# More buffers for the scores of a retrieval layer, its gate loads in thirds, and a softmax exponential one column later

## The reference, cut to what matters

```python
q = (xb @ peer_wq).reshape(PEER_BLOCK, PEER_HEADS, 2, PEER_HALF)
s = jnp.einsum('thpd,pkd->thpk', q, peer_subkeys).astype(jnp.float32)
sv, si = lax.top_k(s, PEER_TOPK)
cand = sv[:, :, 0, :, None] + sv[:, :, 1, None, :]    # 16 x 16 per head
fv, fi = lax.top_k(cand, PEER_TOPK)
eidx = jnp.take_along_axis(cidx, fi, axis=-1)
gate = jax.nn.softmax(fv, axis=-1).astype(xb.dtype)
act = jax.nn.gelu(jnp.einsum('thkd,td->thk', peer_u[eidx], xb))
return jnp.einsum('thk,thkd->td', gate * act, peer_v[eidx])
```

## Time and profile before

| | us |
|---|---|
| median of 3 runs | 4133.24 (4130.62 to 4139.96) |
| the profiled execution | 4130.32 |
| its span, first to last instruction | 4128.6 |
| TensorE busy in it | 3873.2 |
| columns, first to last matmul | 1758.0 to 3008.0 |
| values, first to last matmul | 3008.0 to 4088.0 |

### The profile page before, as it was taken

The page is one execution under the profiler, slowest core; times in us unless marked ns, Lnnn a source line. Parts: engine busy times, 40 slices in busy tenths (PEclk is TensorE's granted clock), DMA queues, the critical chain, the costliest instruction groups (busy, mean ns, idle before and its releaser), DMA issues.

```text
span 4128.6 us, 62540 instructions
## 1 busy us (share of the span) xinstructions
PE 3873.2 (94%) x24143; PEld 3747.4 (91%) x24143; DVE 2592.3 (63%) x3356; ACT 1327.0 (32%) x1620; POOL 806.3 (20%) x514
## 2 busy tenths in 40 slices
PE   8988988979989979999899998999999999999996
PEld 6788978979967979999899998999999999999996
DVE  3423323351363356678888565666898898989896
ACT  3333211132252123232355322222233333333333
POOL 0000010020000020037300021221433233444430
PEclk9989989989999999999999999999999999999998
DMA  6532322223452222234355798999999999999993
GB/s 225 207 115 57 85 60 72 72 60 81 165 222 72 71 62 72 82 127 146 117 194 210 287 348 321 358 343 370 414 406 405 397 393 407 390 402 396 400 377 134
DMA packets 418864, 941.40 MB, mean 228 GB/s; under 512 B 26404, under 2 KB 299488, under 8 KB 366616
## 3 DMA queue, kind: packets, MB, share of 16 engines
q1 hardware_dynamic: 367136, 565.78, 40.4%
q0 software_dynamic: 51616, 374.19, 22.3%
HBM read 865.84 MB, written 72.77 MB: 227 GB/s over the span
## 4 chain that ended last, share of the span: by engine, by line
PE 65%; DMA 16%; DVE 12%; ACT 3%; issue 2%; SPq 2%; DVEq 1%; POOL 0%; ACTq 0%
PE pp L197 25%; PE pp L1134 15%; DMA p_scr<-sa 9%; PE pp L1184 6%; DMA p_f<-p_scr 5%; PE pt L1184 3%; PE pl L1184 3%; DVE gbuf L1926 3%; PE pt L1108 2%; PE pp L809 2%; DVE v_lo L1949 2%; DVE xs_r L1930 1%; PE pt L809 1%; DVE p_lo L1953 1%; PE pl L809 1%
## 5 line engine op out<-in xcount | busy, mean ns | idle before, releaser
L1134 PE MATMUL pp<-h_hi,ut_hi 128*128 128x384 f32 x2048 | 713.1, 348 | 51.8 <-DVE ut_lo L1832 51.2
L1134 PE MATMUL pp<-h_lo,ut_hi 128*128 128x384 f32 x2048 | 698.1, 341 | 0.0
L1134 PE MATMUL pp<-h_hi,ut_lo 128*128 128x384 f32 x2048 | 696.1, 340 | 0.0
L212 DVE TENSOR_TENSOR w_lo<-raw,w_hi 128x2048 fp32r<-128x2048 f32 x120 | 274.7, 2290 | 424.9 <-ACT w_hi L207 424.9
L1832 DVE TENSOR_TENSOR ut_lo<-u_raw,ut_hi 128x1024 fp32r<-128x1024 f32 x256 | 333.0, 1304 | 285.5 <-ACT ut_hi L1415 283.7
L1490 ACT ACTIVATE v_hi<-v_raw 128x1024 fp32r<-128x1024 f32 x256 | 271.9, 1062 | 690.0 <-PE pp L1184 361.0
L1134 PEld LDWEIGHTS pp<-h_hi,ut_hi 128*128 128x128 f32 x2048 | 392.0, 191 | 56.2 <-DVE ut_lo L1832 55.0
L1949 DVE TENSOR_TENSOR v_lo<-v_raw,v_hi 128x1024 fp32r<-128x1024 f32 x256 | 313.0, 1223 | 130.1 <-ACT v_hi L1490 130.0
L1134 PEld LDWEIGHTS pp<-h_lo,ut_hi 128*128 128x128 f32 x2048 | 391.8, 191 | 0.0
L1134 PEld LDWEIGHTS pp<-h_hi,ut_lo 128*128 128x128 f32 x2048 | 390.9, 191 | 0.0
L207 ACT ACTIVATE w_hi<-raw 128x2048 fp32r<-128x2048 f32 x120 | 229.3, 1911 | 419.7 <-PE pp L197 298.2
(11 more groups left out here) (382 smaller groups left out, 7854.1 us busy)
## 6 DMA issues: line engine op xcount, KB each, us to landing
u_raw<-in_peer_ut SPq DMA_DIRECT2D x256, 512.0 KB, 5.6
v_raw<-in_peer_v SPq DMA_DIRECT2D x256, 512.0 KB, 7.9
p_f<-p_scr SPq DMA_DIRECT2D x256, 192.0 KB, 10.7
raw<-in_w_in SPq DMA_DIRECT2D x24, 1024.0 KB, 5.6
g_scr<-gs POOLq DMA_DIRECT2D x6, 4096.0 KB, 13.3
raw<-in_w_mk SPq DMA_DIRECT2D x16, 1024.0 KB, 4.8
raw<-in_w_mv SPq DMA_DIRECT2D x16, 1024.0 KB, 4.8
raw<-in_w_out SPq DMA_DIRECT2D x16, 1024.0 KB, 6.0
```

The source lines that it names most:

```text
L212: nc.vector.tensor_tensor(w_lo[:, s], raw[:, s], w_hi[:, s].bitcast(F32), ALU.subtract).then_inc(lo_ready, 1)
L1134: last = mm(pp[0][:, d, 0:N], w[:, d, k, :], x[:, k, S:S + N], start=(k == 0 and w is ut_hi and x is h_hi), stop=(k == KC - 1 and w is ut_lo))
```

## The change

- fg becomes fs, four buffers in the place of the seventh gather buffer, from column 56 on (columns 0 to 55 keep fg); sa gets four buffers; f_stored and s_in count per buffer. NG_BUF is 6.
- ScalarE has a loop of its own for the gated columns, and waits for the stores of g_scr ahead of it, since fs lies where the last gate tiles were.
- SP's order in a gated column is now: store of sa, first half of u_raw, store of fs, second half of u_raw, load of sa, one stored column further ahead than before (into the buffer whose store was issued a column ago), a third of the gate loads in three columns of four.
- The exponential stands between columns 26 and 27, and VectorE makes the low parts of column 27 ahead of the subtraction, and those of column 28 alone between normalising and the copies.
- The three lists are turned into three banks, with no wait between them.
- Semaphores of GpSimd's memsets are merged into pool_made and const_ready.

```diff
-NG_BUF = 7
+NG_BUF = 6
+        ijt_bank = [pt[0], pt[1], pp[1][:, 0]]
-        sa = at("sa", TMP + 9728, [P, 2, N])
+        fs = at("fs", Y_HI + 49152, [P, 4, N])
+        sa = at("sa", TMP + 6400, [P, 4, N])
...
+            def fours_part(x, q, k, n):
+                for dst, i in ((g4, q),) + (((a4, k),) if k is not None else ()):
+                    sp.dma_start(dst[x][:, 2 * n:2 * n + 2, :, :], gv[i][:, 2 * n:2 * n + 2]).then_inc(g4_in[x], 16)
...
+            def steady(j, d):
+                b = j * 8 + d if isinstance(j, int) else None
+                s, mid = d % 2, b is None
+                if mid or AHEAD + 2 <= b < 2 * AHEAD + 2:
+                    sp.wait_ge(gm_done, j * 16 + (2 * (d - AHEAD) - 2))
+                    sp.dma_start(p_scr[j * 8 + (d - AHEAD - 2)], sa[:, (d - 2) % 4, :]).then_inc(pa_stored[s], 16)
+                if mid or b + 2 < NK:
+                    sp.wait_ge(t_lo, j * 16 + (2 * d + 1))
+                    sp.dma_start(u_raw[:, s, 0:HD], uv[j * 8 + (d + 2)][:, 0:HD]).then_inc(u_in[s][0], 16)
...
+                if mid or AHEAD + 2 <= b < 2 * AHEAD + 2:
+                    sp.wait_ge(gm_done, j * 16 + (2 * (d - AHEAD) - 3))
+                    sp.dma_start(p_scr[j * 8 + (d - 2)], fs[:, (d - 2) % 4, :]).then_inc(f_stored[(d - 2) % 4], 16)
+                elif b >= AHEAD + 2:
+                    p_store(b - 2)
+                if mid or b + 2 < NK:
+                    sp.wait_ge(t_lo, j * 16 + (2 * d + 2))
+                    sp.dma_start(u_raw[:, s, HD:D], uv[j * 8 + (d + 2)][:, HD:D]).then_inc(u_in[s][1], 16)
+                if mid or AHEAD < b < 2 * AHEAD - 1:
+                    if mid or b >= AHEAD + 3:
+                        sp.wait_ge(pa_stored[1 - s], j * 64 + 16 * ((d - 3) // 2 + 1 - AHEAD // 2))
+                    sp.dma_start(sa[:, (d + 1) % 4, :], s_scr[j * 8 + (d - AHEAD + 1)]).then_inc(s_in[(d + 1) % 4], 16)
+                if d % 4 and (mid or b + 4 < NK):
+                    both = mid or b < 2 * AHEAD - 4
+                    fours_part((d // 4 + 1) % 2, j * 2 + (d // 4 + 1),
+                               j * 2 + (d // 4 + 1 - AHEAD // 4) if both else None, d % 4 - 1)
...
             for x in range(3):
                 src = gw if x == 2 else ij[:, x]
-                if x >= 1:
-                    pe.wait_ge(ijt_out, x)
                 for t in range(ND):
-                    last = turn(pt[0][:, t * P:(t + 1) * P], src[:, t + 1, :], ident[:, :])
+                    last = turn(ijt_bank[x][:, t * P:(t + 1) * P], src[:, t + 1, :], ident[:, :])
                 last.then_inc(ijt_done, 1)
-            pe.wait_ge(ijt_out, 3)
...
+            column(PICK // 2 - 1, 0)
             act.wait_ge(g_sub, 1)
             f(gw[:, :, :], gw[:, :, :], ACT.Exp).then_inc(g_exp, 1)
-            for d in range(2):
-                column(PICK // 2 - 1, d)
+            column(PICK // 2 - 1, 1)
...
+            def gated_gelu(q, d):
+                act.wait_ge(u_done, q * 4 + (d + 1))
+                if not isinstance(q, int) or q > AHEAD // 4:
+                    act.wait_ge(f_stored[d], q * 16 + stored(d, -(AHEAD // 4)))
+                f(fs[:, d, :], pp[0][:, d % 2, 0:N], ACT.Gelu_apprx_tanh).then_inc(ge_done, 1)
...
+            for s in range(2):
+                act.wait_ge(g_stored[s], 16 * ND)
+            for d in range(4):
+                gated_column(AHEAD // 4, d)
...
-            def next_rows(count=1, upto=2 * (PICK - 1)):
+            def next_rows(count=1, upto=2 * PICK):
...
-            while turned[0] < 2 * (PICK - 1):
+            while turned[0] < 2 * PICK:
```

More of the change, by code:

```diff
@@ L487, in program, with stored @@
         u_done, ge_done, gm_done = sem("u_done"), sem("ge_done"), sem("gm_done")
-        f_stored = [sem("f_stored0"), sem("f_stored1")]
-        g4_in, s_in, pa_stored = [[sem(f"{w}{s}") for s in range(2)] for w in ("g4_in", "s_in", "pa_stored")]
+        f_stored = [sem(f"f_stored{s}") for s in range(4)]
+        g4_in, pa_stored = [[sem(f"{w}{s}") for s in range(2)] for w in ("g4_in", "pa_stored")]
+        s_in = [sem(f"s_in{s}") for s in range(4)]
+        def stored(s, n):
+            return 16 * n + (8 * AHEAD if s < 2 else 0)
         def gated_count(b):
@@ L708, in ahead_steady @@
[L708 to L736, removed]
+                    for n in range(3):
+                        fours_part(0, AHEAD // 4, 0, n)
@@ L737, in _ @@
+                    for x in range(2):
+                        sp.wait_ge(f_stored[x], 16 * AHEAD // 2)
+                    for q in range(2):
+                        sp.dma_start(sa[:, q, :], s_scr[q]).then_inc(s_in[q], 16)
                 if b == NK - 2:
@@ L739, in _ @@
                         sp.wait_ge(pa_stored[x], 16 * AHEAD // 2)
-                    for d in range(4):
-                        p_load(0, d)
+                    for n in range(4):
+                        p_load(0, n)
                     sp.wait_ge(t_lo, 2 * (NK - 1))
-                    for d in range(2):
[L744 to L749, removed]
+                    for n in range(2):
+                        v_load(0, 0, n)
+                if mid or AHEAD + 2 <= b < 2 * AHEAD + 2:
[14 more added lines that the diff above has]
+                               j * 2 + (d // 4 + 1 - AHEAD // 4) if both else None, d % 4 - 1)
+            for d in range(8):
+                steady(AHEAD // 8, d)
+            with sp.Fori(AHEAD // 8 + 1, AHEAD // 4 - 1) as j:
+                for d in range(8):
+                    steady(j, d)
+            for b in range(2 * AHEAD - 8, NK):
+                steady(b // 8, b % 8)
             sp.wait_ge(t_lo, 2 * NK)
@@ L761, in _ @@
                     value_loads(0, i, d)
-            for s in range(2):
-                sp.wait_ge(f_stored[s], 16 * NK // 2)
+            for s in range(4):
+                sp.wait_ge(f_stored[s], stored(s, (NK - AHEAD) // 4))
             with sp.Fori(AHEAD // 4, NK // 4) as i:
@@ L1458, in _, with gated_column @@
                     column(i, d)
+            column(PICK // 2 - 1, 0)
             act.wait_ge(g_sub, 1)
             f(gw[:, :, :], gw[:, :, :], ACT.Exp).then_inc(g_exp, 1)
-            for d in range(2):
-                column(PICK // 2 - 1, d)
+            column(PICK // 2 - 1, 1)
             for x in range(3):
                 act.wait_ge(ijt_done, x + 1)
-                f(ijt[:, x, :], pt[0][:, 0:N], ACT.Copy).then_inc(ijt_out, 1)
+                f(ijt[:, x, :], ijt_bank[x][:, 0:N], ACT.Copy).then_inc(ijt_out, 1)
             gate_columns(act, column)
-            with act.Fori(PICK // 2 + 4 * ND, GELU_S) as i:
+            with act.Fori(PICK // 2 + 4 * ND, AHEAD // 2) as i:
                 for d in range(2):
                     column(i, d)
+            def gated_gelu(q, d):
[3 more added lines that the diff above has]
+                f(fs[:, d, :], pp[0][:, d % 2, 0:N], ACT.Gelu_apprx_tanh).then_inc(ge_done, 1)
+            def gated_column(q, d):
+                for h in range(2):
+                    x = (d + 1) % 2
+                    act.wait_ge(u_in[x][h], q * 32 + 16 * ((d + 1) // 2 + 1))
+                    act.wait_ge(u_done, q * 4 + d)
+                    f(ut_hi[:, x, 8 * h:8 * h + 8, :], u_raw[:, x, h * HD:(h + 1) * HD].rearrange("p (c i) -> p c i", c=8),
+                      ACT.Copy).then_inc(t_hi, 1)
+                gated_gelu(q, d)
+            for s in range(2):
+                act.wait_ge(g_stored[s], 16 * ND)
+            for d in range(4):
+                gated_column(AHEAD // 4, d)
+            with act.Fori(AHEAD // 4 + 1, GELU_S // 2) as q:
+                for d in range(4):
+                    gated_column(q, d)
             act.wait_ge(step_done, U_0)
             f(wrs[:, :], s_s[:, :], ACT.Gelu_apprx_tanh).then_inc(s_ge, 1)
[L1472 to L1475, removed]
+            with act.Fori(GELU_S // 2, NK // 4 - 1) as q:
+                for d in range(4):
+                    gated_column(q, d)
+            for d in range(3):
+                gated_column(NK // 4 - 1, d)
             def v_split(s, i, d):
@@ L1501, in _ @@
                 p_split(0, 0, d)
-            gelu(NK // 2 - 1, 1)
+            gated_gelu(NK // 4 - 1, 3)
             for d in range(2, 4):
```

62 lines of the change are left out of this document (23 added, 39 removed).

## The result

The changed kernel took **4077.28 us** in the median of 4 runs (4073.78 to 4082.29), against 4132.01 (4130.62 to 4139.96) for the kernel before: a ratio of 0.9866, with a 95% interval of 0.9852 to 0.988. That is 54.7 us less, where 4082 was forecast.

What follows compares the result with a forecast made beforehand. TensorE, stalled in columns 56 to 111 by late stores and then slowed by the low clock, was taken as the bound; 45 us there plus 5 at the softmax from 4130.3, with half of 3 us added, gave 4082, range 4061 to 4107.

Steps and rivals of the forecast that it cites:

- Rival A: Gated columns 56 to 111: TensorE alone bounds them, stage falls to 463.5 us, kernel to 4066; chance 0.22.
- the floor of the DMA engines: Columns 56 to 111: moving 182 MB bounds the stage between 463.5 and 487 us, taken as 478.
- the forecast's own case: Columns 56 to 111 fall from 522.9 to 478 us, limited by the DMA engines, gaining 45 us; chance 0.58.
- the order on SP's queue: Gated columns: store of sa first puts the first half of u_raw 1 to 1.5 us later, costing nothing.
- The softmax: Near column 27: the stall moves behind that column, 9.3 us instead of 11.7; gain 5 us, bounds 0 and 8.
- The clock: TensorE in the gated columns: low clock cost about 20 us; long stalls are paid a second time, short ones not.
- six gather buffers: Values stage: six buffers give 28 us, less about 4, against gathers landing in 7.6 to 11.9 us; covered.
- the wait for g_scr: ScalarE's new wait for these stores, ahead of the gated columns, costs nothing; the gathers wait for the same stores.
- the issue of more loads: SP's queue in gated columns: gates in three parts take 0.4 us more issuing per column, costing nothing.
- Rival B: Gated columns: the DMA is full already, 182 MB take 497 us, kernel 4101; chance 0.14.
- Rival C: Gated columns: the last third of the gates lands late and VectorE stands, slower at 4171; chance 0.03.
- D: Gated columns: loads of u_raw, not the buffers, set the stall, so nothing moves, 4130; chance 0.03.

Runs made afterwards that it cites:

- e7: Changed kernel with one more unread 128 KB load per column in columns 57 to 111, 4% more bytes there: 4078.41 us, ratio 0.9875.
- e8: Changed kernel with two more unread 128 KB loads per column in columns 57 to 111, 8% more bytes there: 4093.65 us, ratio 0.9906.
- e9: Changed kernel with gelu's and SP's waits for stores both as with two buffers, and gate loads issued whole: 4089.87 us, ratio 0.9883.
- e2: Changed kernel with SP waiting, before each load of sa, for its own store of sa as with two buffers: 4093.82 us, ratio 0.9898.
- e10: Changed kernel with only SP's wait for its store of sa as with two buffers, and gate loads issued whole: 4079.47 us, ratio 0.9871.
- e3: Changed kernel with gelu waiting for the store of two columns back, as with two buffers: 4075.67 us, ratio 0.9855.
- e11: Changed kernel with only gelu's wait for its store as with two buffers, and gate loads issued whole: 4070.16 us, ratio 0.9844.
- e5: Changed kernel with the exponential ahead of column 26 again, low parts of column 27 after it, three banks kept: 4077.46 us, ratio 0.9864.
- e6: Kernel before with six gather buffers instead of seven and nothing else: 4136.14 us, ratio 1.0003.
- e1: Changed kernel with a block's gate loads issued whole in one column again, four buffers kept: 4073.76 us, ratio 0.9843.
- e4: Changed kernel with both gelu's and SP's waits for stores as with two buffers, gate loads still in thirds: 4097.2 us, ratio 0.9908.

## Why the prediction was right, and where it was not

**The place and the size.** That the time lies in the 55 gated columns, that the low clock there goes with the stalls, and that nothing is left of the waits for stores came out as forecast. 4077.3 lies in the range and 4.7 us from the forecast. That it lies so near is in part luck. From gelu to gelu the columns gained 61.6 us (60.1 + 3.3 - 1.8) where 50 were forecast; the medians differ by 54.7, and against the 4135.2 to 4140.0 of the kernel before in the later sets it would be 58 to 63. Rival A's own figure was 4066.

**The term that was mis-sized** is the floor of the DMA engines, "between 463.5 (TensorE alone) and 487 ... I take 478". The stage gained 59.4 us by the windows of the earlier trace rows, not 45: rival A (0.22) is what happened, not the forecast's own case. Two mistakes were in it. Scaling by the share of packet time (497 us at 1.02 are 487) takes that share for work, yet the changed kernel moved the same bytes in 463.5 us at the same share of 1.02, that is in 473 us of packet time; why packets took longer before was not tested. And the 386 to 388 GB/s of the earlier trace rows were the demand of those columns at TensorE's pace, not a ceiling; e7 and e8 found the ceiling at 403 to 404. That the 358 GB/s of the Trainium skill (DMA: Bandwidth & Descriptors, Specifications) does not hold here was rightly read: 392 GB/s stood for 463.5 us.

**The cause was given to the wrong parts.** The prediction put the stall down to two buffers each behind bursts of gate loads. By the tables above the fs buffers bring nothing by themselves, and the thirds nothing in the stretch and a small loss over columns 56 to 127. With the new order in place the sa buffers bring 14 to 16 us (18 to 19 with those of fs), and 41 come from what e9 keeps: the order on SP's queue, the earlier load and the gate loads in pieces. The prediction had priced the order at "Nothing" from a single side: it saw that the half panel goes out later by 1 to 1.5 us and not that the store of sa, on which SP stands, goes out ahead of 512 KB. The reading of the earlier trace rows, that SP stands for its own store with everything queued behind it, held: put back alone, SP's wait costs 14 to 16 us (e2, e10) and gelu's nothing (e3, e11).

**The softmax.** The forward working held to 0.2 us: a stall of 9.3 us was forecast and 9.13 came; with the first column 6.8 us later in this execution, the first gate matrix was due at 2022.2 and came at 2022.09. Yet the gain was 3.3 us, not 5: the first gate matrix came 5.4 us sooner, but the working stopped there and left out that the low clock lasts beyond it. A matmul at 2026.20 still takes 0.52 us, 9 us after the stall's end, and that slows column 28. The banks, counted in, gave nothing (e5).

**The clock.** From the earlier trace rows the prediction had it that short stalls are not paid a second time. The kernel before already shows otherwise: behind an idle time of 1.80 us (restart at 2838.02) matmuls take 0.53 us from 2839.1 to 2841.7, while 1.79 us ahead of 2571.05 left no mark. It did no harm to the forecast, since no wait was left in the stretch.

**Costed at nothing and so found:** six gather buffers (e6), the wait for g_scr (column 56 came without idle time), the issue of more loads within the stretch. Rival B fell with the 392 GB/s. Rival C never showed: VectorE has no wait for gates in the stretch. D fell with the result.

**What was not in the sum:** columns 112 to 127 are 1.8 us longer. With the same bytes in whole loads they take 134.8 us (e1, e11), as before, so this goes with the thirds.

## What to carry to other kernels

On a queue in order, look first at what the issuing engine itself stands for: give a wait for one's own store as much time as can be, by an earlier store, an earlier load or a spare buffer. Here what e9 kept of the new order and the earlier load gave 41 us, and the buffers 18 to 19 on top. A rate seen at full pace is a demand, not a ceiling; only more bytes show the ceiling. And waits of an engine with time to spare, summed, do not price a stall: here ScalarE waited 224 us for stores in a kernel whose TensorE idled 8.5 in that window, and 234 us in one whose TensorE idled 39.5. What is split for smoothness should be measured by itself: the thirds gave nothing.

## What the runs showed of the hardware that was not expected

- 1.5 MB of loads per block more or less in one go make no difference to a core that draws 392 GB/s, as long as nobody waits for what stands behind them (e1: 463.5 us either way, and 134.8 against 136.4 in the columns behind).
- The share of packet time does not add up to work: 0.95 went with 348 GB/s, 1.02 with 392, 1.04 with 404, all with nearly the same mix.
- The low clock outlasts a stall by more than I had counted: after 11.66 us idle the matmuls were at full speed again 5 us after the restart, after 9.13 us only after about 9, where the engine had worked with gaps in between (turnings, a wait of 0.8 us for the one-hot pair). Idle times of 1.8 to 3 us are followed by slow matmuls in some places (before at 2838.02, e4 at 2732.86: 0.53 and 0.52 us instead of 0.34) and not in others (before at 2571.05).
- 4% more bytes cost nothing in the stretch that carries them; the next one took 139.9 us instead of 135.7 to 137.0 (e7).
